# A two-layer hybrid decoder step on eight cores: 32 blocks a core, transposes by DMA, and a new order of the steps around the norms

## The reference

```python
h = rmsnorm(x, g_pre_mix)
hc, bg, cg, up, q, k, v, gc, gp, ga = jnp.split(h @ w_in, SPLIT_IDX, axis=-1)   # w_in (1024, 8704)
conv_out, conv_new = short_conv(cg * hc, conv_past, conv_w)       # causal, width 3
y_conv = (bg * conv_out) @ w_conv_out
pooled, pool_new = multiscale_pool(up, pool_past, start)          # trailing means over 2, 4, 8, 16 positions
y_pool = grouped(pooled @ w_pool) * pool_scale                    # 4 groups of 256 channels
attn = swa_banded(rope(q), rope(k), v, sinks)                     # 128 queries read their own and the previous 128 keys
y_attn = attn @ w_attn_out
merged = sigmoid(gc) * y_conv + sigmoid(gp) * y_pool + sigmoid(ga) * y_attn
x = x + rmsnorm(merged @ w_mix_out, g_post_mix)
f = jnp.square(relu(rmsnorm(x, g_pre_mlp) @ w_up)) @ w_down       # 1024 -> 4096 -> 1024
x = x + rmsnorm(f, g_post_mlp)
```

## Time and profile before

| | us |
|---|---|
| median of 3 runs | 5234.58 |
| lowest, highest | 5229.73, 5278.91 |
| the profiled execution | 5279.87 |
| its span on the slowest core (core 0) | 5278.8 |
| spans of the 8 cores | 5214.2 to 5278.8 |

### The profile page before, as it was taken

How to read it: one execution, slowest core, us unless ns; L and a number is a source line. 1 busy time by engine, 2 the same in 40 slices (tenths; PEclk the granted TensorE clock), 3 DMA queues, 4 the chain that set the end, 5 groups by cost and what they waited for, 6 DMA issues and landing times.

```text
span 5278.8 us, 87954 instructions; the slowest of 8 cores (5214.2 to 5278.8 us)
## 1 busy us (share of the span) xinstructions
PE 5027.6 (95%) x29282; PEld 2630.1 (50%) x29282; DVE 2618.1 (50%) x4529; ACT 1890.5 (36%) x3840; POOL 658.0 (12%) x1412
## 2 busy tenths in 40 slices
PE   6999999899999999999999999999999999999999
PEld 3544455445544554445444544454445445654654
DVE  3553266326641665166516661566156615643662
ACT  2423234323432343234323432343234323442441
POOL 1001100111011101110101011101010101011011
PEclk8889999999999999999999999999999999999999
DMA  7656786673221322231222222322222224332332
GB/s 178 147 139 133 174 188 156 119 192 112 73 88 68 101 83 84 92 132 69 92 73 84 92 81 92 132 74 75 100 84 78 75 97 154 102 116 88 122 111 73
DMA packets 156442, 570.79 MB, mean 108 GB/s; under 512 B 18528, under 2 KB 21120, under 8 KB 155584
## 3 DMA queue, kind: packets, MB, share of 16 engines
q0 software_dynamic: 114624, 418.43, 28.8%
q1 hardware_dynamic: 41088, 146.47, 7.8%
q10 hardware_dynamic: 288, 0.26, 0.0%
HBM read 550.91 MB, written 111.48 MB: 125 GB/s over the span
## 4 chain that ended last, share of the span: by engine, by line
PE 82%; DVE 6%; DMA 4%; issue 4%; ACT 3%; POOL 1%; DVEq 0%; SPq 0%; ACTq 0%; POOLq 0%
PE ps L384 81%; ACT scr L391 3%; DVE tm L404 2%; PE ps L388 1%; DMA wslot<-wts 1%; DMA sk_o<-ck 1%; DMA x<-xin 1%; DVE scr L394 1%; DVE x L394 1%; DMA y<-tm 1%; DVE scr L404 1%; POOL rs L394 1%; DVE hT L394 1%; DVEq L85 0%; POOL rs L400 0%
## 5 line engine op out<-in xcount | busy, mean ns | idle before, releaser
L384 PE MATMUL ps<-hT,wslot 128*128 128x512 bf16 (+2 forms) x15680 | 3009.0, 349 | 73.2 <-DVE hT L394 60.1
L384 PEld LDWEIGHTS ps<-hT,wslot 128*128 128x128 bf16 x15680 | 1538.3, 99 | 1401.3 <-issue 228.8
L391 ACT ACTIVATE scr<-ps 128x512 bf16<-128x512 f32 (+6 forms) x2110 | 1272.0, 605 | 2502.2 <-PE ps L384 2244.0
L384 PE MATMUL ps<-wslot,big 128*128 128x512 bf16 (+1 forms) x5440 | 1219.6, 384 | 39.0 <-DVE big L404 39.0
L384 PEld LDWEIGHTS ps<-wslot,big 128*128 128x128 bf16 (+1 forms) x5440 | 528.2, 99 | 696.6 <-issue 108.5
L394 DVE TENSOR_TENSOR big<-scr 128x384 bf16<-128x384 bf16 (+5 forms) x800 | 336.8, 423 | 676.1 <-ACT scr L391 598.9
L134 POOL DMA_DIRECT2D wslot<-wbf x632 | 337.8, 535 | 2670.8 <-PE ps L384 2637.2
L384 PE MATMUL ps<-big,wslot 128*128 128x384 bf16 (+2 forms) x2880 | 609.3, 349 | 1.2 <-DVE scr L404 1.1
L404 DVE SCALAR_TENSOR_TENSOR tm<-scr,rs,gpost 128x512 f32<-128x512 f32 x68 | 50.9, 749 | 744.5 <-POOL rs L394 717.7
L384 PEld LDWEIGHTS ps<-big,wslot 128*128 128x128 bf16 x2880 | 272.0, 99 | 250.8 <-issue 53.9
L394 DVE TENSOR_TENSOR scr<-ps,ropeT 128x384 f32<-128x384 f32 (+2 forms) x400 | 231.5, 593 | 188.2 <-PE ps L384 182.1
(11 more groups left out here) (84 smaller groups left out, 2418.0 us busy)
## 6 DMA issues: line engine op xcount, KB each, us to landing
wslot<-wbf POOLq DMA_DIRECT2D x632, 512.0 KB, 4.4
wslot<-wts POOLq DMA_DIRECT2D x158, 512.0 KB, 15.1
wbf<-wslot SPq DMA_DIRECT2D x158, 512.0 KB, 11.0
x<-xin SPq DMA_DIRECT2D x33, 512.0 KB, 5.3
y<-tm SPq DMA_DIRECT2D x33, 512.0 KB, 5.3
gpost<-norm_post_mix SPq DMA_DIRECT2D x10, 512.0 KB, 5.0
gpost<-norm_post_mlp SPq DMA_DIRECT2D x10, 512.0 KB, 4.8
sk_o<-ck SPq DMA_DIRECT2D x8, 508.0 KB
```

Of the source, the lines that this page charges most:

```text
L384: return S.op("pe", lambda e: e.matmul(out, lhsT, rhs, start=start, stop=stop, **kw), reads=reads, writes=writes, signal=signal)
L391: return S.op("act", lambda e: e.activation(out=out, in_=in_, func=func, **kw), reads=reads, writes=writes)
```

## The change

The changed kernel differs in these things.

- **Blocks.** A core owns 32 blocks. Two context blocks lie ahead of them (zeros for the first core of a sequence). Of the first, "block A", layer 0 computes only keys and values, and the last 16 positions of its hT (`HALO`) for hc, cg and up. The second is block slot 0 of tile 0: complete in layer 0, keys, values and 16 positions in layer 1. Tile 0 has groups of 3 and 4 blocks in layer 0, and of 3 and 3 in layer 1. The state of conv and pooling at the start is no longer zero but comes from the halo columns; the mask of the first block is multiplied by `pflag` (0 or 1).
- **Transposes.** Outside tile 0 `turn` issues a DMA transpose from SyncE in place of the TensorE transposes, for hT (128x1024) and for attention (128x512). The gain is then multiplied into hT in place. Tile 0 keeps TensorE (`by_pe`), except for the rows of tile 1 that are loaded at its end.
- **Chains.** The product with `gpost` is made straight from the PSUM bank, ahead of rstd; one VectorE instruction then multiplies by rstd and adds x. In the down-projection the first half's sum of squares and product are made for all rows between the halves. `mix_row` runs over chunks 0 to 4 and then 5 to 7 of the merged rows, each chunk with its own record (`OTC`), with a tick after each part. There are more ticks in `up_chunks`, and a tile's first norm comes one yield earlier.
- **Queues.** The bf16 pieces are loaded by SyncE instead of GpSimd, five ticks after release. At the start only 6 pieces are issued ahead of the first norms, and the x of group B is issued ahead of `ropeT`, after piece 2 instead of piece 3.

```diff
+    def dma_turn(self, dsem, out, in_, reads=(), writes=()):
+        self._deps("sp", reads, writes)
...
+        inst = self.eng["sp"].dma_start_transpose(out=out, in_=in_)
...
-            S.dma("pool", wsem[s], wslot[s][:, :], wbf[l, n, :, :], reads=[wbfB[l][n]], writes=[wB[s]])
+            S.dma("sp", wsem2[s], wslot[s][:, :], wbf[l, n, :, :], reads=[wbfB[l][n]], writes=[wB[s]])
...
-    def pump(lag=3):
-        store_pieces(2 if wstate["n"] < len(pieces) // len(tiles) else 0)
+    def pump(lag=None):
+        store_pieces(8 if wstate["n"] < len(pieces) // len(tiles) else 0)
         while wstate["n"] < len(pieces):
             prev = wstate["n"] - nslot
-            if prev >= 0 and (prev not in released or released[prev] + lag > wstate["age"]):
+            if wstate["n"] >= wstate["cap"]:
+                break
+            wait_ = lag if lag is not None else 3 if wstate["n"] < len(pieces) // len(tiles) else 5
+            if prev >= 0 and (prev not in released or released[prev] + wait_ > wstate["age"]):
                 break
...
+        turn(hT[:, :, col:col + np_], htm.h[0:np_, 0:D], [htm.b], [hTS[slot]])
+        htm.free()
         yield
         yield
...
+        tt("dve", hT[:, :, col:col + np_], hT[:, :, col:col + np_],
+           gT[:, l, :].unsqueeze(2).to_broadcast([128, 8, np_]), ALU.mult, [hTS[slot], gB], [hTS[slot]])
...
         r, rB = rstd(ssT, ssB, np_, 4.0)
+        while not tmidle:
+            yield
+        ix = tmidle.pop(0)
+        tm, tmB = TM.t[:, ix, :], TM.b[ix]
+        tt("dve", halves(tm[0:np_, :]), pap, halves(gpost[0:np_, :]), ALU.mult, pbufs + [gpostB], [tmB])
+        banks.put(b0, b0 + 1)
         yield
-        tm, tmB = TM.get()
-        stt(halves(tm[0:np_, :]), pap, r[0:np_, :], halves(gpost[0:np_, :]), ALU.mult, ALU.mult,
-            pbufs + [rB, gpostB], [tmB])
-        banks.put(b0, b0 + 1)
-        tt("dve", x[0:np_, slot, :], x[0:np_, slot, :], tm[0:np_, :], ALU.add, [xB[slot], tmB], [xB[slot]])
+        stt(x[0:np_, slot, :], tm[0:np_, :], r[0:np_, :], x[0:np_, slot, :], ALU.mult, ALU.add,
+            [tmB, rB, xB[slot]], [xB[slot]])
+        tmidle.append(ix)
...
+    def down_half(np_, bk, i, ss, ssB, out, outB):
         junk = scr.get()
...
+        act(junk.h[0:np_, 0:512], ps[0:np_, bk, :], AF.Square, [pB[bk]], [junk.b, ssB], accum_out=ss[0:np_, i:i + 1])
         junk.free()
+        tt("dve", out, ps[0:np_, bk, :], gpost[0:np_, i * 512:(i + 1) * 512], ALU.mult, [pB[bk], gpostB], [outB])
+        banks.put(bk)
...
+        down_half(np_, bk, 1, ss, ssB, tm[0:np_, 512:1024], tmB)
...
+        for i, (src, b_) in enumerate(((st.f[0:np_, 0:512], st.b), (tm[0:np_, 512:1024], tmB))):
+            cs = slice(i * 512, (i + 1) * 512)
+            stt(dst[0:np_, cs], src, r[0:np_, :], x[0:np_, slot, cs], ALU.mult, ALU.add,
+                [b_, rB, xB[slot]], [dstB])
...
-            for _ in range(4):
+            for _ in range(3):
                 yield
...
-    def proj(wt, wBuf, cols, g, among=None):
+    def proj(wt, wBuf, cols, g, among=None, halo=0):
         bk = banks.get(among)
         for k in range(8):
-            mm(ps[:, bk, 0:g.nt], cols(wt, k), hT[:, k, g.c0:g.c0 + g.nt],
-               k == 0, k == 7, [wBuf, hTB[g.gi]], [pB[bk]], signal=(k == 7))
+            mm(ps[:, bk, 0:halo + g.nt], cols(wt, k), hT[:, k, g.c0 - halo:g.c0 + g.nt],
+               k == 0, k == 7, [wBuf] + [hTS[i] for i in g.slots] + (g.hsrc if halo else []), [pB[bk]], signal=(k == 7))
...
+        turn(V["QT"][:, 4 * p:4 * p + 4, col:col + 128], On.h[:, 0:512], [On.b], [ATB[slot][p]])
         On.free()
...
+            for p in range(2):
+                bq = banks.get()
+                for k in range(8):
+                    mm(ps[:, bq, 0:128], wk[:, k, p * 128:(p + 1) * 128], hh[:, k, :], k == 0, k == 7,
+                       [wkB] + hhB, [pB[bq]], signal=(k == 7))
...
-            for cgi in range(2):
-                for c in range(8):
-                    wm, wmB = weight(ti, l, "wmix", (cgi, c // 4))
...
-                       [wmB, OTB[g.gi]], [pB[b0 + cgi]], signal=(c == 7))
...
+            for cs in ((0, 1, 2, 3, 4), (5, 6, 7)):
+                for cgi in range(2):
+                    for c in cs:
+                        wm, wmB = weight(ti, l, "wmix", (cgi, c // 4))
...
+                           [wmB, OTC[g.gi][c]], [pB[b0 + cgi]], signal=(c == 7))
+                tick()
...
+            down_half(np_, bk, 0, ss, ssB, st.f[0:np_, 0:512], st.b)
...
+            if ti == 0 and l > 0:
+                szs, b = (3, 3), 1
...
-FULL_TILES = [((4, 3), False), ((4, 3), False), ((4, 3), False), ((4, 3), False), ((3, 2), True)]
+FULL_TILES = [((3, 4), False), ((4, 3), False), ((4, 3), False), ((4, 3), False), ((3, 2), True)]
```

More of the change, by code:

```diff
@@ L225, with __init__ @@
 class Group:
-    def __init__(self, gi, blocks, c0, ns, first_chain):
+    def __init__(self, gi, blocks, c0, ns, halo=0, f0=None, hsrc=()):
         self.gi = gi
@@ L232, in __init__ @@
         self.nt = self.n + ns
-        self.first_chain = first_chain
+        self.halo = halo
+        self.f0 = f0
+        self.hsrc = list(hsrc)
+        self.slots = [slot for slot, cb in blocks]
+        if ns:
+            self.slots.append(blocks[-1][0] + 1)
 def build_program(nblk, tiles, with_samples=True, depth=2, nslot=12, nscr=11):
@@ L240, in build_program @@
     NBS = max(sum(sizes) + (2 if (hs and with_samples) else 0) for sizes, hs in tiles)
-    TT = max(128 * sum(sizes) + (NS if hs else 0) for sizes, hs in tiles)
-    TTs = [128 * sum(sizes) + (NS if (hs and with_samples) else 0) for sizes, hs in tiles]
+    off = [HALO] + [0] * (len(tiles) - 1)
+    TTs = [o_ + 128 * sum(sizes) + (NS if (hs and with_samples) else 0) for o_, (sizes, hs) in zip(off, tiles)]
+    TT = max(TTs)
     def din(name, shape, dt=F32):
@@ L561, in build_program @@
     loads = []
-    b0_ = 0
-    for sizes, hs in tiles:
+    b0_ = 1
+    for ti_, (sizes, hs) in enumerate(tiles):
         starts.append(b0_)
@@ L1000, in layer, with fin @@
         wv, wvB = weight(ti, l, "kv", 1)
+        if groups[0].halo:
+            if l == 0:
+                hh, hhB, other = hAv, [hA.b], (128, ropeAv, ropeA.b)
+            else:
+                hh, hhB, other = hT[:, :, HALO:HALO + 128], [hTS[0]], (128, ropeT[:, :, HALO:HALO + 128], ropeB)
+            for p in range(2):
[3 more added lines that the diff above has]
+                       [wkB] + hhB, [pB[bq]], signal=(k == 7))
+                def fin(t1, t2, p=p):
+                    tt("dve", KTp[l][:, p, :], t1.f[:, 0:128], t2.f[:, 0:128], ALU.add, [t1.b, t2.b], [KTpB[l]])
+                ru = rope_unit(bq, None, fin, other)
+                next(ru)
+                if pend is not None:
+                    run(pend)
+                pend = ru
+            bv = banks.get()
+            for k in range(8):
+                mm(ps[:, bv, 0:256], hh[:, k, :], wv[:, k, :], k == 0, k == 7, [wvB] + hhB, [pB[bv]], signal=(k == 7))
+            cp("act", Vp[l][:, :, 0:64], ps[:, bv, 0:256].rearrange("p (h e) -> p h e", h=4), [pB[bv]], [VpB[l]])
+            banks.put(bv)
+            run(pend)
+            pend = None
+            if l == 0:
+                hA.free()
+                ropeA.free()
@@ L1037, in layer @@
         apair = (4, 6)
-        units = [attn_unit(l, g, bi, p, apair) for g in groups for bi in range(len(g.blocks)) for p in range(2)]
+        units = [attn_unit(ti, l, g, bi, p, apair) for g in groups for bi in range(len(g.blocks)) for p in range(2)]
         live = []
@@ L1068, in layer @@
             step_attn(True)
-        S.alias(QTB, OTB)
+        for g in groups:
+            S.alias([QTB[g.gi]], [b_ for i in g.slots for b_ in ATB[i]])
         nb = sum(tiles[ti][0])
@@ L1095, in layer @@
             load_rope(ti + 1)
+        for g in groups:
+            S.alias([QTB[g.gi]] + [b_ for i in g.slots for b_ in ATB[i]], OTC[g.gi])
         def gp_unit(i, g, among=None):
@@ L1140, in layer @@
         gp_some(8)
+        assert not todo
         done(ti, l, "wpool", 0)
@@ L1177, in layer, with tag @@
             done(ti, l, "wup", i)
+        def tag(g, slot):
+            return int(slot > 3) if ti == 0 else g.gi
+        if ti == 0 and l == L - 1:
+            S.alias(list(hTS), hTS)
+            load_x(1, loads[1][0])
+            chains.append((0, chain_norm(0, 128, gpreT, kB["gpre"], 0, 0, loads[1][0][3])))
         pbk = [banks.get() for _ in rows]
@@ L1331 @@
     wts = pack_weights(inp)
-    vec = host_vec(inp)
+    vec = [host_vec(inp, h) for h in range(2)]
     in_maps = []
```

331 lines of the change are left out of this document (186 added, 145 removed).

## The result

The changed kernel takes **0.962 of the time before, with a 95% interval of 0.950 to 0.974**; its profiled run took 5048.16 us, and where it was measured a second time, beside the first three experiments, the ratio was 0.964 (0.960 to 0.968) and the time 5044 us. Forecast was 4968 us, in a range of 4905 to 5110. The direction was right, and the time lies inside the range, but 80 us above the forecast. (Runs in which one die had a lower clock are left out of all ratios.)

The account below looks back on a forecast made before the run. TensorE was taken as the bound, busy 5027.6 of 5278.8 us. Terms -74 + 8 - 71 - 87 - 8 - 22 - 12 - 1 = -267 from the median 5234.58 gave 4968 us, range 4905 to 5110.

Parts of the forecast that it names:

- One block-layer less: Layer 1 on a core: 32 blocks instead of 33, saving one block's TensorE busy time, -74 us.
- Halo and block A: Tile 0: extra products and rotations for the halo and block A, plus short waits, +8 us (6 to 12).
- Transposes: TensorE outside tile 0: 1264 transposes fewer at 0.056 us each, -71 us.
- s = 5: Time from issue to landing of a 128x1024 DMA transpose (256 KB), taken as 5 us, ends 3.5 and 10.6.
- Start: Kernel start: with six pieces and x ahead of the rope table, group B's rows land sooner, -12 us (-18 to +3).
- Idle time of tiles 1 to 4: TensorE's waits there, 163 us before: 46 left at joints and 30 in small gaps and sample attention, -87 us.
- Clock: Clock dips at the joints of four tiles: part of the lost clock comes back, -22 us (-5 to -34).
- Queues: GpSimd's 632 issues go to SyncE, which has little else; later release costs little of the lead: nothing.
- end most of the 3.1: Wmix-to-wup joint: product ahead of rstd and no bank for transposes end most of TensorE's 3.1 us wait.
- joints half cured: Joints of tiles 1 to 4: s is 7.5 or banks run short another way, time 5045 us; chance 0.22.
- The expected signs: Profile after: 328 TensorE transposes, no last-gate waits in tiles 1 to 4, idle near 130 us, seven-block layer about 510.
- the three signs of being wrong: Transposes over 7 us in a row; VectorE's waits for them leaving TensorE without banks; weight pieces late behind SyncE's waits.

Follow-up runs that it names:

- the first three experiments: Block-layer left out of the kernel before: 0.988; changed kernel with all transposes on TensorE: 0.969; changed kernel with weight pieces on GpSimd's queue again: 0.968.
- the three edits of order: Changed kernel with samples' key/value loads gated in the last tile, next-tile gains two ticks later, and at most one weight piece per tick: 0.949, 4961 and 4966 us.
- the block experiment: Kernel before, with the first block not computed in layer 1 of tile 0: 0.988, 5166 and 5168 us.
- the combined kernel: Changed kernel with gated samples' loads, later gain and paced weight pieces together: 0.949, 4961 and 4966 us.
- the two with TensorE's transposes: Changed kernel with all transposes on TensorE, without the three edits of order (5064 to 5071 us) and with them (5073 us twice).
- The gate: Changed kernel; last tile's loads of samples' keys and values wait until VectorE has written group B's q of the first two rounds: 0.9615, 5026 to 5031 us.
- the pacing: Changed kernel with at most one weight piece issued per tick in tiles 1 to 4: 0.959, 5013 to 5020 us.

## Why the prediction was right, and where it was not

The direction was right, and the range was wide enough to hold a rival's 5045; the sum itself was 80 us off. All of the miss lies in tiles 1 to 4. On core 6 tile 0 takes 1131 us before and 1047 after, 84 less, where my terms for it make 86. The other tiles take 4086 and 3983, 103 less, where mine make 181 (71, 87, 22 and 1). With the three edits of order they take 3903, 184 less.

By its own terms, in us (measured against 5230 before):

- *One block-layer less, -74*: -64. TensorE's part was near (67 to 71), the rest came back as waits.
- *Halo and block A, +8*: TensorE is busy 530.3 us in tile 0's layer 0 after, and 521 to 532 on the cores of the block experiment, whose layer 0 is the old one: -2 to +9. So 8 is at the upper end of what these stretches allow, and they don't fix it closer.
- *Transposes, -71*: on TensorE 75 to 80, between the combined kernel (4792.6) and the two with TensorE's transposes (4867.6 and 4872.6), all three at a clock of 0.988 to 0.990. They are 1280 transposes, not 1264. Right, as was the choice of the smaller price.
- *s = 5*: 3.1 by itself. Of the two pages of the Trainium skill, "VectorE: DVE Perf Modes", section "The three transpose paths", has 1309 ns for one tile; eight in a row would be an estimated 10.5 us, and by the 3.1 measured they do not follow each other at that price. The 261 GB/s in the Trainium skill's "DMA: Bandwidth & Descriptors", section "Latency and other measured facts", an estimated 1.0 us for 256 KB beside a fixed part, fits the 3.1, though no run measures the two parts. But s is no constant: 7.5 us behind four weight pieces, 17 beside 2 MB of the samples' state.
- *Start, -12*: group B's first transposes come at 47.34 in place of 64.27; the wait ahead of them is 11.36 in place of 19.59. Right in the main.
- *Idle time of tiles 1 to 4, 163 to 76*: **this is the step that failed.** The eight windows of core 2 sum to 143 (with 9 at the very end left out). With the three edits those of core 6 sum to 75 and those of the slowest core to 77, about the number forecast. So the cover that I counted is there, but only if a transpose really takes 3 to 5 us and its gain stands where it has landed.
- *Clock, -22*: nothing on cores 4 to 7, 0.984 before and after. With the edits, and idle time gone, it is 0.990. In these runs the term moves with the one above.
- *Queues, "Nothing"*: **the larger part of the cause of the failed step.** I asked what the 632 issues do to SyncE and to TensorE's lead, and both were as I said. I did not ask what GpSimd's queue does once they have left it, nor what a burst of pieces does to a transpose behind it. The gate gives 17 us and the pacing 28. The rest of the cause is the place of the gain in VectorE's order: I named the wait there, and counted it as covered; two ticks later it gives 23. Together the three edits give 80, and the forecast was 80 off.

Part of the nearness is luck, since inside the idle term a second size was wrong as well. The order of the row steps, with the product ahead of the power, was a half sentence of mine ("end most of the 3.1"); undoing it costs 104 us here, more than the whole idle term. Without it the forecast would have missed by 184 in place of 80. Whether the DMA transposes made the joints so sensitive to it, or it would bring as much with TensorE's transposes, was not tried.

The busy time closes within what can be read: between like clocks it fell by 144 to 156, and block, halo and transposes measured one by one make 133 to 153. The 45 us by which core 0 was longer than the median before lie in tile 0's layer 0, 646 us there where cores 5 to 7 have 584 to 589, so no term had to carry them. The rival *joints half cured* (5045) names the right time. Its first condition, s near 7.5 for all transposes, did not come; only those in company are that slow. Its second, banks that run short in another way, is close to what the last tile shows.

The expected signs came out so: 328 transposes on TensorE, tile 0's layer 1 in 464 (said: 470), a seven-block layer in 519 (said: 510), no end of the waits for the last gate (19.5 left, 16.8 of them in tiles 1 to 4), idle time of 235 in place of 130. Of the three signs of being wrong one is there in part: at the last tile VectorE's wait for a transpose leaves TensorE without a bank for 16.20 us. No piece came late. Ten of the 108 transposes for hT took over 7 us, and one of them with the three edits.

## What to carry to other kernels

When issues leave a queue, look at what stood behind them: the queue was pacing it, and a load that is suddenly free to run will find the one moment at which a short transfer is waited for. When work moves from an engine to a DMA queue, its latency is set by the transfers issued just ahead of it, and by everything in flight; spread the large ones, and put the consumer's step in its in-order engine only where the transfer has surely landed. And the order within a short chain of row steps can be worth as much as the large work beside it (104 us here, with 110 for the transposes in the best order): undo each part by itself before crediting the one with the big name.

## What was not expected of the hardware

- The issue of a DMA transpose of 128x1024 holds SyncE for 1.2 us in the median and 1.34 in the row above, where four weight pieces take 1.91 together. Beside 2 MB in flight it held it for 6.24 us.
- The same 632 loads of 512 KB, issued from GpSimd's queue instead of SyncE's, slow the DMA transposes of 128x1024 from a median of 3.1 to 3.6 us, though their own count and size are the same.
- TensorE with more work and less idle time ran at a higher clock: with 1280 more transposes its mean granted clock was 0.990 against 0.983 and its idle time 199 us against 235 (slowest cores), and its busy time rose by 55.6 us only, not by the 75 that the same transposes cost between kernels of one clock.
